# Normalising attention's outputs instead of its probabilities, and making the cell's gate rows later, in one kernel

## The chip, the cores and the metric

One Trainium2 chip, one core of it. The metric is the device time of one execution of the whole program, in microseconds; the median of the runs counts. All arithmetic is float32.

## The reference

Two blocks of two layers each work on 512 tokens of width 1024; the first block has 256 context tokens besides. A layer of the first block has three branches (a depthwise convolution of width 31, a gated linear attention, a grouped softmax attention) that are merged; a layer of the second block is an mLSTM cell and a retention in chunks. The parts that the change touches:

```python
def gqa_attend(q, k, v):
    s = jnp.einsum('bqkgd,bskd->bkgqs', q, k).astype(jnp.float32) * (ATT_HD ** -0.5)
    p = jax.nn.softmax(s, axis=-1).astype(v.dtype)
    return jnp.einsum('bkgqs,bskd->bqkgd', p, v)
...
    li = gate_chunks(i_pre.astype(jnp.float32))
    lf = gate_chunks(jax.nn.log_sigmoid(f_pre.astype(jnp.float32)))
...
        b = jnp.cumsum(lfj, axis=-1)
        a = b + m[..., None]
        g = b[..., :, None] - b[..., None, :] + lij[..., None, :]
...
        m_row = jnp.maximum(a, jnp.max(g, axis=-1))
        w_intra = jnp.exp(g - m_row[..., None])
```

Attention has 8 query heads and 2 key heads of width 64; the 512 latent tokens look at 768 keys, and in layer 0 the 256 context tokens look at their own 256. The gate rows are what the cell needs of i and f for its four heads along the 512 tokens: running sums, running maxima and their differences.

## The kernel before

Each engine has a program of its own (tensor, scalar, vector, gpsimd, sync), written out in order by hand. A wait names an event by a key (`at(("probs", i, e))`); a first pass of the program counts at which value of which semaphore the event happens. Every operation of VectorE and of GpSimd that goes through `link` waits for its own end. ScalarE's functions all go through line 1089, most of VectorE's through lines 1483 to 1489, so that the trace shows these helpers' lines and not the callers'.

PSUM has 8 banks of 128 x 512 floats. `claim` waits until the last reader of a bank has freed it. Weights come through a ring of four slots of 1 MB, loaded by the sync engine as slots are used up; attention uses none.

**Attention** (`attend`, lines 657, 1197 and 1638) walks over pairs: one pair is 128 queries of two heads e = 0, 1. Layer 0 has 8 pairs of context (256 keys, one half) and 16 of latents (768 keys, two halves of 384); layer 1 has the 16 of latents. Banks are taken by parity: pair i has banks 4(i mod 2) to 4(i mod 2)+3, one for each head and half. A round n does scores of pair n (L677, heads on different rows of TensorE), transposes of the probabilities of pair n-1 (L690) into the banks that held its scores, and values of pair n-2 (L711, heads on different columns) into columns 384 to 512 of a bank of the other parity. VectorE takes the negated maximum of a head's scores (L1651); ScalarE makes exponentials with it as bias, and their sum by the side (shown as a read of its accumulator); VectorE takes the reciprocal (L1489) and multiplies the probabilities by it (L1485), and only then does TensorE transpose. ScalarE copies three of the four transposed halves and the output from PSUM (L1089), VectorE the fourth (L1488). TensorE's order is: scores, transposes of head 0, values of the pair before, transposes of head 1. ScalarE's order is: copy (0,1), exponential of head 0, copy (0,0), output copy, copy (1,0), exponential of head 1.

Beside this, **GpSimd** convolves: 31 taps, each a multiply by a column (L1966) and an addition (L1967), for four tiles and in layer 0 for two segments. TensorE's first work after attention is the sum over the convolution's channels (`csum`, through L419), which waits for the whole convolution (`("conv", l)`, line 860). After attention VectorE multiplies all heads by their gate (line 1727), which waits for `("att out", l)`.

**The second block** has for each layer and head four or five groups of products (`steps2`, `products` and `corners`, lines 950 to 976): a 1024 x 256 weight load is multiplied in seven quarter-sized products of sums. `products` is four of them; VectorE then makes U2 from two results (line 1874) and W2 and the corner c22 (lines 1876 and 1892); `corners` (three products) waits for U2 and c22. After corners VectorE adds U2 to two quarters (lines 1897 to 1911). All of these products are at L947. GpSimd makes the sums of weights (`pair_sums`, L2003 to L2006), each set waiting for the corners of two groups before, and for the cell's heads a four-tap convolution (`taps`, L2019, L1966, L1967).

Ahead of all groups a narrow product with the gate weights is made (`("if", l)`, L435). **ScalarE** takes it from PSUM with two biases, then absolute value, exponential and logarithm (lines 1389 to 1395), and **VectorE**, which has just made the sums of h (lines 1802 to 1805), waits for the logarithm and makes the gate rows (lines 1806 to 1818): one two-input operation, two scans, four two-input operations and a small copy, all on 4 partitions of 512. TensorE wants the rows at `gate_cols` (line 920), after the fifth group of head 0. In VectorE's order the gate rows stand before the U2 of group (0, 0).

```python
                for n in range(len(pairs) + 1):
...
                    if n < len(pairs):
                        for e in range(2):
                            z = 2 * (i % 2) + e
                            eng.wait_ge(*at(("probs", i, e)))
                            rcp(small[:, 48 + z:49 + z], small[:, 44 + z:45 + z])
                            ts(pr[:, z, 0:halves * w], pr[:, z, 0:halves * w], small[:, 48 + z:49 + z], None, M_, None,
                               ("probs norm", i, e))
```

## Time and profile before

| | |
|---|---|
| runs | 3575.69, 3580.43, 3581.15 us; median 3580.43 |
| the profiled execution | 3579.02 us, its span 3577.0 us |
| busy: PE / DVE / ACT / POOL | 3259.3 / 1339.7 / 833.6 / 1433.7 us |
| chain that ended last | PE 73%, POOL 15%, DVE 7%, issue 3%, ACT 2% |
| attention of layer 0, first scores to the column sums | 583.86 to 739.72 us |
| attention of layer 1, first scores to the column sums | 1669.11 to 1770.65 us |
| second block, first groups of its layers | 2145.65 and 2872.76 us |

PE is TensorE's matmuls, PEld its weight loads, DVE VectorE, ACT ScalarE, POOL GpSimd. Times count from the span's start. A float32 matmul shows as two instructions, a transpose as one. The chain that ended last is followed back from the last instruction; its parts on POOL are the convolution's end of layer 0 and GpSimd's share at the beginning of the second block's layers. Where a timeline row has brackets at its end, the engine stood still for so long before it, and what follows the arrow is what ended the wait.

### The profile page before, as it was taken

What the parts mean: (1) busy time and instruction counts of PE and PEld (TensorE: products, weight loads), DVE (VectorE), ACT (ScalarE), POOL (GpSimd) and SP (SyncE); (2) the same over time, 40 slices, a digit from 0 to 9 for tenths busy, and PEclk for the clock granted to TensorE, in tenths of its full rate; (3) what the DMA queues carried; (4) which work ended last, traced back from release to release, by engine and by line L of the source; (5) the groups of instructions that cost most, each with busy time, mean ns of one, the idle gap of its engine ahead of it and who ended that gap; (6) DMA issues with size and microseconds to landing.
All of it is one profiled execution on the core that took longest, in us unless ns stands there. A gap on an engine that the chain in (4) does not pass through costs nothing.

```text
span 3577.0 us, 38442 instructions
## 1 busy us (share of the span) xinstructions
PE 3259.3 (91%) x14397; PEld 2221.3 (62%) x14397; DVE 1339.7 (37%) x2454; ACT 833.6 (23%) x1487; POOL 1433.7 (40%) x1372
## 2 busy tenths in 40 slices
PE   5999897779999989987899979999999889999998
PEld 4666564546665546454544437888986378889953
DVE  6211314724444231225632242555552234444322
ACT  2312323611111031323521112222121023221110
POOL 0008988920000000899200016667651166775600
PEclk6999997989999999998999989999999999999998
DMA  6111110003222111210034412322331321222211
GB/s 193 47 36 36 30 36 13 2 24 97 92 88 91 50 57 47 53 36 24 1 112 124 130 52 71 94 84 83 107 106 36 84 71 60 71 71 71 71 46 48
DMA packets 259178, 236.47 MB, mean 66 GB/s; under 512 B 20870, under 2 KB 257202, under 8 KB 258996
## 3 DMA queue, kind: packets, MB, share of 16 engines
q1 hardware_dynamic: 258996, 234.02, 21.5%
q8 instruction: 117, 1.92, 0.2%
q14 instruction: 65, 0.53, 0.0%
HBM read 231.90 MB, written 2.10 MB: 65 GB/s over the span
## 4 chain that ended last, share of the span: by engine, by line
PE 73%; POOL 15%; DVE 7%; issue 3%; ACT 2%; DMA 0%; DVEq 0%; ACTq 0%; SPq 0%; POOLq 0%
PE ps L419 33%; PE ps L947 20%; POOL arena L1967 8%; PE ps L449 8%; POOL posi L1966 4%; PE ps L997 2%; DVE arena L1483 2%; ACT arena L1089 1%; PE ps L435 1%; PE ps L1041 1%; DVE arena L1487 1%; PE ps L1033 1%; DVE bQz L1487 1%; PE ps L515 1%; DVE arena L1485 1%
## 5 line engine op out<-in xcount | busy, mean ns | idle before, releaser
L419 PE MATMUL ps<-hT,wring 128*128 128x512 f32 (+1 forms) x1568 | 579.2, 530 | 1.4 <-ACT arena L1089 1.4
L419 PE MATMUL ps<-arena,wring 128*128 128x512 f32 (+1 forms) x1280 | 489.9, 543 | 10.6 <-DVE arena L1483 10.6
L419 PEld LDWEIGHTS ps<-hT,wring 128*128 128x128 f32 x1568 | 303.5, 195 | 261.0 <-issue 244.9
L2003 POOL TENSOR_TENSOR arena<-wring 128x512 f32<-128x512 f32 x72 | 93.2, 1294 | 867.7 <-DMA wring<-in_w_in 561.8
L1967 POOL TENSOR_TENSOR arena<-arena,posi 128x512 f32<-128x512 f32 (+1 forms) x360 | 409.2, 1137 | 30.0
L449 PE MATMUL ps<-hT,wring 128*128 128x512 f32 (+1 forms) x1088 | 403.9, 525 | 0.0
L419 PEld LDWEIGHTS ps<-arena,wring 128*128 128x128 f32 x1280 | 242.7, 191 | 246.6 <-issue 227.2
L1089 ACT ACTIVATE arena<-ps 128x256 f32<-128x256 f32 (+4 forms) x447 | 194.1, 434 | 747.8 <-PE ps L419 324.9
L449 PEld LDWEIGHTS ps<-hT,wring 128*128 128x128 f32 x1088 | 205.8, 194 | 162.6 <-issue 153.3
L1089 ACT ACT_TABLE_LOAD x146 | 187.3, 1283 | 492.1 <-PE ps L527 95.2
L1483 DVE TENSOR_TENSOR arena<-arena 128x768 f32<-128x768 f32 (+7 forms) x121 | 158.2, 1307 | 363.4 <-ACT arena L1089 360.5
L1089 ACT ACTIVATE arena<-ps,cols 128x512 f32<-128x512 f32 (+2 forms) x186 | 113.4, 610 | 717.4 <-PE ps L419 404.0
L1966 POOL TENSOR_SCALAR posi<-arena,cols 128x512 f32<-128x512 f32 (+1 forms) x360 | 250.4, 695 | 35.4
L947 PE MATMUL ps<-hT,wring 128*128 128x256 f32 x896 | 228.3, 401 | 26.4 <-DVE posi L1483 26.2
L1979 POOL TENSOR_TENSOR arena<-arena 128x512 f32<-128x512 f32 (+1 forms) x12 | 13.1, 1092 | 521.4 <-ACT arena L1089 520.6
L1487 DVE SCALAR_TENSOR_TENSOR bQz<-wring,cT,bQz 128x256 f32<-128x256 f32 x392 | 213.9, 546 | 14.0
L947 PE MATMUL ps<-hT,arena 128*128 128x256 f32 x896 | 213.1, 381 | 0.0
L947 PE MATMUL ps<-xT,wring 128*128 128x256 f32 x896 | 211.7, 379 | 0.0
L947 PEld LDWEIGHTS ps<-hT,wring 128*128 128x128 f32 x896 | 175.8, 202 | 54.8 <-DVE posi L1483 29.2
L947 PEld LDWEIGHTS ps<-hT,arena 128*128 128x128 f32 x896 | 171.9, 192 | 24.0
L947 PEld LDWEIGHTS ps<-xT,wring 128*128 128x128 f32 x896 | 170.2, 190 | 23.1
L1973 POOL MEMSET arena<- 128x60 f32 x8 | 1.2, 151 | 447.1 <-DVE arena L1483 446.5
(184 smaller groups left out, 4300.9 us busy)
## 6 DMA issues: line engine op xcount, KB each, us to landing
wring<-in_w_in SPq DMA_DIRECT2D x128, 1024.0 KB, 5.3
wring<-in_w_mod SPq DMA_DIRECT2D x24, 1024.0 KB, 7.7
wring<-in_w_out SPq DMA_DIRECT2D x24, 1024.0 KB, 5.7
wring<-in_w_ada SPq DMA_DIRECT2D x24, 1024.0 KB, 5.2
wring<-in_w_conv_out SPq DMA_DIRECT2D x8, 512.0 KB, 3.6
wring<-in_w_gla_out SPq DMA_DIRECT2D x8, 512.0 KB, 4.0
wring<-in_w_attn_out SPq DMA_DIRECT2D x8, 512.0 KB, 4.0
arena<-in_x SPq DMA_DIRECT2D x1, 2048.0 KB, 9.6
```

The source lines that it names most:

```text
L419: last = eng.matmul(o_(out), a, b_, start=(i == 0), stop=(i == len(parts) - 1))
L435: mm = eng.matmul(bank[b][0:M, 0:n], w[:, k, 0:M], hT[:, k, t0:t0 + n], start=(k == 0), stop=(k == KD - 1))
L449: mm = eng.matmul(bank[b][:, 0:n], w[:, k, j * P:(j + 1) * P], hT[:, k, t0:t0 + n], start=(k == 0), stop=(k == KD - 1))
L515: last = eng.matmul(o_[:, c:c + 1], (md2 if L > 2 else md_first if (L, g) < (0, 8) else md)[:, i, c * 256 + j * P:c * 256 + (j + 1) * P], ...
L947: mm = eng.matmul(o_, lhs, rhs, start=first and u == 0 and k == 0, stop=k == 3, skip_group_check=True)
L997: eng.matmul(bank[7 - j][:, 0:TX], w_out[j][:, k, :], ys[:, k, :], start=(k == 0), stop=False)
L1089: act.link(eng.activation(out_, in_, func, **kw), key)
L1483: tt = lambda o_, a, b, op, key=None: dve.link(eng.tensor_tensor(o_, a, b, op), key)
L1487: eng.scalar_tensor_tensor(out=o_, in0=a, scalar=s_, in1=b, op0=op0, op1=op1), key)
L1966: pool.link(eng.tensor_scalar(scratch, src, w, 0.0, ALU.mult, ALU.add))
L1967: pool.link(eng.tensor_tensor(dst, dst, scratch, ALU.add))
L2003: pool.link(eng.tensor_tensor(t1, w[:, 0:4, P:2 * P], w[:, 0:4, 0:P], ALU.subtract))
```

## The change

Two parts in one kernel.

*Attention.* Probabilities are transposed and multiplied with the values as the exponentials are. VectorE makes one reciprocal of both heads' sums a pair. In the middle of the values of a pair, after the second tile of keys, TensorE spreads the reciprocals over a head's 64 rows by a product with the identity, into the neighbouring bank; VectorE copies this from PSUM (128 x 128), waits for the values and multiplies the output by it on its way out of PSUM, in place of ScalarE's copy. TensorE's order becomes scores, all four transposes, values; scores are made with half 1 first, and banks are claimed half by half. The values' bank is claimed, since it holds the transposes just made. ScalarE's order becomes three copies, two exponentials.

*Gate rows.* ScalarE's five functions stand after its copy for the corners of load (0, 0), VectorE's eight operations after the c22 of load (0, 1).

```diff
@@ tensor
+        osum = sq[1][:, 0:P]
...
-                    claim(b0, b0 + 1, b0 + 2, b0 + 3)
...
-                    for half in range(halves):
+                    for half in range(halves - 1, -1, -1):
+                        claim(b0 + half, b0 + 2 + half)
...
-                    eng.wait_ge(*at(("probs norm", i, e)))
+                    eng.wait_ge(*at(("probs", i, e)))
...
+                    claim(b)
                     g = hp // 2
                     for kt in range(halves * w // P):
                         for e in range(2):
                             last = eng.matmul(bank[b][rows_of[e], 384:512], av[:, kt, g * 64:(g + 1) * 64],
                                               pt[:, 2 * (i % 2) + e, kt * P:(kt + 1) * P],
                                               start=(kt == 0), stop=(kt == halves * w // P - 1))
+                        if kt == 1:
+                            claim(b + 1)
+                            eng.wait_ge(*at(("shares", i)))
+                            for e in range(2):
+                                z = 48 + 2 * (i % 2) + e
+                                spread = eng.matmul(bank[b + 1][rows_of[e], 384:512], small[:, z:z + 1].broadcast_to([P, 64]),
+                                                    ident, start=True, stop=True)
+                            spread.then_inc(*pe.tell(("full", part)))
...
                     if 1 <= n <= len(pairs):
-                        halves = key_halves(pairs[n - 1][0])[0]
-                        for half in range(halves - 1, -1, -1):
-                            turn(n - 1, 0, half, half > 0 or n == 1)
+                        for e in range(2):
+                            for half in range(key_halves(pairs[n - 1][0])[0]):
+                                turn(n - 1, e, half)
                     if n >= 2:
                         values(n - 2)
-                    if 1 <= n <= len(pairs):
-                        for half in range(halves):
-                            turn(n - 1, 1, half, True)
@@ scalar, attend
+                for n in range(len(pairs) + 1):
+                    if n:
+                        for half in range(key_halves(pairs[n - 1][0])[0]):
+                            turned(n - 1, 0, half)
+                        turned(n - 1, 1, 0)
                     if n < len(pairs):
                         probabilities(n, 0)
                         probabilities(n, 1)
@@ scalar, corners of the second block
                         if not r and i:
                             silu(n, i - 1)
+                        if (n, i) == (0, 0):
+                            gate_rows()
@@ vector, attend, after the maxima of pair n
+                    if 1 <= n <= len(pairs):
+                        if key_halves(pairs[n - 1][0])[0] > 1:
+                            k = ("pT", i - 1, 1, 1)
+                            eng.wait_ge(*at(("full", k)))
+                            cp(pt[:, 2 * ((i - 1) % 2) + 1, 384:768], bank_of[k][:, 0:384], ("free", k))
+                        z = 2 * ((i - 1) % 2)
+                        eng.wait_ge(*at(("probs", i - 1, 1)))
+                        rcp(small[:, 48 + z:50 + z], small[:, 44 + z:46 + z], ("shares", i - 1))
+                    if n >= 2:
...
+                        eng.wait_ge(*at(("full", part)))
+                        cp(osum, bank_of[part][:, 384:512], ("free", part))
                         eng.wait_ge(*at(("full", k)))
+                        tt(res[:, 8 + hp, q0:q0 + P], bank_of[k][:, 384:512], osum, M_, ("free", k))
@@ vector, products of the second block
                         tt(c22, d_, w_, A_, ("c22", k))
+                        if (n, i) == (0, 1):
+                            gate_rows()
```

## Rows read from the trace of the kernel before

**Rows 1.** Timeline, end of layer 0's attention: start us, us, engine, line, shapes, count, wait.

```profile
739.72 8.12 PE L419 MATMUL ps<-arena,const 128*128 128x512 f32 x16 [25.03 <-POOL arena L1967]
```

**Rows 2.** Groups by shape, GpSimd, 611 to 708 us: count, busy us, mean ns, idle.

```profile
L1967 POOL TENSOR_TENSOR arena<-arena,posi 128x512 f32<-128x512 f32 x30 | 40.3, 1343 | 2.5
L1966 POOL TENSOR_SCALAR posi<-arena,cols 128x512 f32<-128x512 f32 x30 | 22.9, 763 | 2.9
```

**Rows 3.** The same view, GpSimd, from 745 us to the end (second block).

```profile
L1967 POOL TENSOR_TENSOR arena<-arena 128x512 f32<-128x512 f32 x96 | 121.9, 1270 | 8.0
...
L1966 POOL TENSOR_SCALAR arena<-arena,cols 128x512 f32<-128x512 f32 x96 | 66.8, 696 | 9.3
```

**Rows 4.** Timeline, layer 1's attention: scores of rounds 3 and 15, column sums.

```profile
1689.73 1.56 PE L677 MATMUL ps<-arena 64*128 64x384 f32 x8 [1.03 <-DVE small L1489]
...
1758.86 1.56 PE L677 MATMUL ps<-arena 64*128 64x384 f32 x8 [1.03 <-DVE small L1489]
...
1770.65 3.70 PE L419 MATMUL ps<-arena,const 128*128 128x512 f32 x8
```

**Rows 5.** Timeline, one round of layer 1's attention.

```profile
1724.78 1.56 PE L677 MATMUL ps<-arena 64*128 64x384 f32 x8 [1.03 <-DVE small L1489]
...
1725.70 0.62 DVE L1485 TENSOR_SCALAR arena<-arena,small 128x768 f32<-128x768 f32 x1
...
1726.27 0.87 PE L690 MATMUL ps<-const,arena 128*128 128x128 f32 x6
1726.41 1.95 DVE L1651 TENSOR_REDUCE small<-ps 128x1 f32<-128x768 f32 x2
1726.91 0.49 ACT L1089 ACTIVATE arena<-ps 128x384 f32<-128x384 f32 x1 [1.51 <-PE ps L690]
...
1727.07 1.53 PE L711 MATMUL ps<-arena 128*64 128x128 f32 x24
1727.46 0.90 ACT L1089 ACTIVATE arena<-ps,small 128x768 f32<-128x768 f32 x1
...
1728.53 0.88 PE L690 MATMUL ps<-const,arena 128*128 128x128 f32 x6
1728.71 1.32 ACT L1089 ACTIVATE arena<-ps 128x384 f32<-128x384 f32 x3 [0.26 <-PE ps L711]
1729.51 0.56 DVE L1488 COPY arena<-ps 128x384 f32<-128x384 f32 x1 [1.16 <-PE ps L690]
```

**Rows 6.** Timeline, first groups of the second block's layers.

```profile
2145.82 1.40 ACT L1089 ACTIVATE arena<-ps,small 4x512 f32<-4x512 f32 x2 [4.26 <-PE ps L435]
...
2151.85 0.68 DVE L1487 SCALAR_TENSOR_TENSOR arena<-arena 4x512 f32<-4x512 f32 x1 [5.15 <-ACT arena L1089]
...
2158.58 3.52 PE L947 MATMUL ps<-hT,wring 128*128 128x256 f32 x8 [5.76 <-DVE posi L1483]
...
2165.73 1.29 POOL L2003 TENSOR_TENSOR arena<-wring 128x512 f32<-128x512 f32 x1 [48.91 <-PE ps L947]
...
2219.74 0.72 ACT L1089 ACTIVATE arena<-arena,cols 128x512 f32<-128x512 f32 x1 [3.29 <-POOL arena L1967]
...
2885.82 3.42 PE L947 MATMUL ps<-hT,wring 128*128 128x256 f32 x8 [5.89 <-DVE posi L1483]
```

**Rows 7.** Chain that ended last: start us, us, what.

```profile
2232.61 5.18 PE ps L947 x24
```

**Rows 8.** Windows of layer 1's attention: busy us by engine, PEclk, DMA share, GB/s.

```profile
1668.00:1690.00 22.00, 15.35 (x74) 9.98 (x76) 15.87 (x22) 10.11 (x19) 20.28 (x20) 0.64 0.00 1
...
1720.00:1765.00 45.00, 36.18 (x349) 26.03 (x346) 32.16 (x56) 29.75 (x64) 0.00 (x0) 1.00 0.00 1
```

**Rows 9.** Timeline, gate of layer 0's linear attention, GpSimd and VectorE.

```profile
399.99 2.13 DVE L1549 TENSOR_TENSOR_SCAN arena<-gscan,arena 128x768 f32<-128x768 f32 x1
400.60 2.57 POOL L1967 TENSOR_TENSOR arena<-arena,posi 128x512 f32<-128x512 f32 x1
```

More of the change, by code:

```diff
@@ L678, in scores, with turn @@
                                               ak[r, hp // 2, half * w:(half + 1) * w], start=True, stop=True)
-                            if half == halves - 1:
+                            if half == 0:
                                 last.then_inc(*pe.tell(("scores", i, e)))
-                def turn(n, e, half, tell):
+                def turn(n, e, half):
                     i = first + n
@@ L691, in turn @@
                                              pr[:, 2 * (i % 2) + e, half * w + u * P:half * w + (u + 1) * P], ident)
-                    if tell:
-                        last.then_inc(*pe.tell(("full", key)))
+                    last.then_inc(*pe.tell(("full", key)))
                 def values(n):
@@ L698, in values @@
                     halves, w = key_halves(sg)
-                    key = ("o", i)
+                    key, part = ("o", i), ("shares", i)
                     b = 4 * ((i + 1) % 2)
-                    if n == len(pairs) - 1:
-                        claim(b)
-                    bank_of[key], last_on[b] = bank[b], key
                     for e in range(2):
@@ L713, in values @@
                                               start=(kt == 0), stop=(kt == halves * w // P - 1))
-                    last.then_inc(*pe.tell(("full", key)))
-                    if n < len(pairs) - 1:
-                        m.mark(("full", ("pT", i + 1, 0, 0)), *m.at[("full", key)])
+                        if kt == 1:
[6 more added lines that the diff above has]
+                            spread.then_inc(*pe.tell(("full", part)))
+                    if halves > 1:
+                        last.then_inc(*pe.tell(("full", key)))
+                    else:
+                        m.mark(("full", key), *m.at[("full", part)])
+                    bank_of[key], bank_of[part] = bank[b], bank[b + 1]
+                    last_on[b], last_on[b + 1] = key, part
                 for n in range(len(pairs) + 2):
@@ L1218, in turned @@
                     evac(("pT", i, e, half), pt[:, 2 * (i % 2) + e, half * w:(half + 1) * w], 0, w)
-                def output(n):
-                    sg, hp, qb = pairs[n]
-                    q0 = SEG[sg][0] + qb * P
-                    evac(("o", first + n), res[:, 8 + hp, q0:q0 + P], 384, P)
-                for n in range(len(pairs) + 2):
-                    before = key_halves(pairs[n - 1][0])[0] if 1 <= n <= len(pairs) else 0
-                    if before == 2:
-                        turned(n - 1, 0, 1)
+                for n in range(len(pairs) + 1):
[3 more added lines that the diff above has]
+                        turned(n - 1, 1, 0)
                     if n < len(pairs):
                         probabilities(n, 0)
-                    if before:
-                        turned(n - 1, 0, 0)
-                    if n >= 2:
-                        output(n - 2)
-                    if before:
-                        turned(n - 1, 1, 0)
-                    if n < len(pairs):
                         probabilities(n, 1)
-                m.mark(("att out", l), *m.at[("free", ("o", first + len(pairs) - 1))])
             for l in range(DEPTH):
@@ L1642, in attend @@
                 att_no[0] += len(pairs)
-                for n in range(len(pairs) + 1):
+                for n in range(len(pairs) + 2):
                     i = first + n
@@ L1651, in attend @@
                             dve.link(eng.tensor_reduce(small[:, 40 + z:41 + z], src, ax, ALU.max, negate=True), ("nmax", i, e))
-                    if n and key_halves(pairs[n - 1][0])[0] > 1:
-                        k = ("pT", i - 1, 1, 1)
-                        eng.wait_ge(*at(("full", k)))
-                        cp(pt[:, 2 * ((i - 1) % 2) + 1, 384:768], bank_of[k][:, 0:384], ("free", k))
-                    if n < len(pairs):
-                        for e in range(2):
-                            z = 2 * (i % 2) + e
-                            eng.wait_ge(*at(("probs", i, e)))
-                            rcp(small[:, 48 + z:49 + z], small[:, 44 + z:45 + z])
-                            ts(pr[:, z, 0:halves * w], pr[:, z, 0:halves * w], small[:, 48 + z:49 + z], None, M_, None,
-                               ("probs norm", i, e))
+                    if 1 <= n <= len(pairs):
[7 more added lines that the diff above has]
+                    if n >= 2:
+                        sg, hp, qb = pairs[n - 2]
+                        q0 = SEG[sg][0] + qb * P
+                        k, part = ("o", i - 2), ("shares", i - 2)
+                        eng.wait_ge(*at(("full", part)))
+                        cp(osum, bank_of[part][:, 384:512], ("free", part))
+                        eng.wait_ge(*at(("full", k)))
+                        tt(res[:, 8 + hp, q0:q0 + P], bank_of[k][:, 384:512], osum, M_, ("free", k))
+                m.mark(("att out", l), *m.at[("free", ("o", first + len(pairs) - 1))])
             for l in range(DEPTH):
```

44 lines of the change are left out of this document (24 added, 20 removed).

## Prediction

> **What bounds the kernel now.** I read three places: the windows for what each engine does in a stretch, the timeline of one round of each loop that the diff touches, and the timeline where the next stage picks up. What decides there is which wait ends last, not which engine is busy.
>
> Attention of layer 0 is not on the path. When it ends, TensorE stands still for 25.03 us until GpSimd has finished the depthwise convolution; the column sums start at 739.72 [rows 1]. The path there is GpSimd's, and the normalising multiplies of VectorE slow it: while they run, its 512-wide multiply takes 763 ns and its 512-wide add 1343 ns [rows 2], against 696 and 1270 ns later, with no such neighbour [rows 3].
>
> Attention of layer 1 is on the path: its column sums follow the last values at 1770.65 without a gap [rows 4]. One round of it shows what sets its pace [rows 5]. TensorE has scores from 1724.78, the transposes of the even head from 1726.27, values from 1727.07, the transposes of the odd head from 1728.53, together 4.61 us, and then waits for about 1.0 us; the round lasts 5.65. The ring that closes it is ScalarE's exponential of the odd head (0.90 and 0.19 for its sum), VectorE's reciprocal and multiply (0.16, 0.62), the maximum of the next pair (half of 1.95), the exponential of its even head (1.1), and the three copies that stand before the odd one in ScalarE's order (1.32): 5.3 us before any signalling. The multiply stands in this ring. While GpSimd still convolves, multiply and GpSimd lengthen each other, so the mean of the 12 rounds from 1689.73 to 1758.86 is 5.76 us [rows 4].
>
> In both layers of the second block VectorE makes the gate rows, from 2151.85, ahead of the sum U2 that TensorE's first corner product needs; TensorE waits 5.76 us and restarts at 2158.58, slowly: eight matmuls in 3.52 us, 24 until 2165.57 [rows 6]. At full clock such 24 take 5.18 [rows 7]. When they end GpSimd starts on the third load (2165.73) and is at work until it releases ScalarE at 2219.74 [rows 6]. The second layer is the same, with 5.89 us waited [rows 6].
>
> **The change, part by part.**
> 1. *Layer 1's attention.* Out of VectorE go two multiplies and one of two reciprocals a pair; in come a copy and a product of 128x128 from PSUM. Neither form is in the trace; the 128x384 copy takes 0.56 [rows 5], so each lies between a third of that, 0.19, and the whole. I take 0.3. VectorE then has 1.95 + 0.56 + 0.16 + 0.6 = 3.3 us of work a round; ScalarE loses its output copy (0.28 or so of the 1.32) and has 1.04 + 0.5 + 2.2 = 3.7. TensorE gains four half instructions of the value kind: 24 of these take 1.46 us [rows 5], so 0.24 (bounds 0.2 and, with their own signalling, 0.5). Its work is 4.61 + 0.24 = 4.85.
>  New waits: values now wait, after all four transposes, for ScalarE's copies of the first two. The copy of the first starts 0.64 after the transposes do, as now [rows 5], and takes 0.49, so 1.1, plus up to 0.35 of signalling; the four transposes take 1.6. The second copy is done at 1.65 and is wanted at 1.6 + 0.5 = 2.1. Both are hidden, if ScalarE has finished its exponentials by then; it has more than 1 us to spare. Queued behind this wait are the next scores. These now wait for VectorE's copy of the spread sums: maxima end 2.1 after the transposes' start, then odd-head copy 2.7, reciprocal 2.9, spread copy 3.2, with signalling 3.4 to 3.6, against the values' end at 3.3. That is 0.1 to 0.3 of stall. The product that frees the output bank ends at 3.9 and is covered by the first half of the scores (0.75). Exponentials end at 4.2 and the next transposes begin at 5.1: hidden. So the ring is now TensorE's own: 4.85 + 0.2 stall + 0.15 for the break in the middle of values = 5.2 us, bounds 4.9 and 5.5. Twelve rounds: 12 x (5.76 - 5.2) = 6.7 us.
>  Head: the transposes of pair 0 start without reciprocal and multiply, 1.2 us earlier for the second head (two of 0.16 + 0.62, less what the exponential between them takes), and the first slow rounds carry 1.5 in all. The granted clock is 0.64 there [rows 8], so TensorE's added work costs double and I do not take more. Tail: no multiply before the last transposes, an added product after the last values that the column sums don't need: 1.3. Together 9.5 us (bounds 5 and 13).
> 2. *Layer 0's attention.* Its own shortening, some 12 us, buys nothing: TensorE would wait 37 instead of 25 us. What is gained is GpSimd's time: 30 x (1343 - 1270) ns + 30 x (763 - 696) ns = 4.2 us [rows 2, 3]; with the 256-wide operations in the last third of the stretch, for which I add a quarter, 5.3 (bounds 3 and 6). The new VectorE operations read PSUM; I charge GpSimd nothing for them.
> 3. *Gate rows.* At their old place they cost the wait and the slow restart. Moved, U2 is ready when the first four product groups end (2158.58 - 5.76 = 2152.82), the corner ends 5.18 later at 2158.0 instead of 2165.57: 7.5 us earlier, and GpSimd's chain with it. ScalarE's five gate functions with two table loads take 6.0 us, from 2145.82 to where VectorE starts on their result [rows 6]; from 2154.9, after the corner's first copy, they end at 2160.9, and the next group needs ScalarE at 2161.5. VectorE's now stand ahead of the corner sums of load 1, which free a bank wanted only ten us later.
>  But they now run beside GpSimd, which is the path there. Beside a scan of 2.13 us GpSimd's addition of 1.27 took 2.57, so it lost 0.61 of VectorE's time [rows 9, 3]. Gate rows are 6.2 us of such operations (2151.85 to 2158.1), but on 4 partitions; rows show no price for so few. Bounds: nothing, and all of the 6.2. By the scan's share it would be 3.8; I take 3.4, since half of them are shorter operations with a gap behind each. Net 7.5 - 3.4 = 4.1 to 4.2, in two layers 8.3 (bounds 2.6 and 15).
>  The Trainium skill (GPSIMD Engine Reference, Specifications) says the SBUF interfaces are shared with VectorE, with contention from VectorE instructions in a 2-port mode or with two SBUF inputs. By that rule the removed multiplies help and the moved gate rows hurt, which [rows 2, 3, 9] bear out; it gives no size.
>
> **Sum.** 9.5 + 5.3 + 8.3 = 23.1. The profiled execution took 3579.0 (span 3577.0), 1.4 below the median of 3580.4; from the median that is 3557.
>
> **Rivals.**
> - *GpSimd pays for the gate rows in full.* The moved rows cost it 5.5 to 7.5 us a layer, since VectorE is also slowed and the moved group grows to 9 us. Then part 3 gives 0 to 4 and the time is 3561 to 3566. For: GpSimd is on the path throughout [rows 6, 9]. Against: only four partitions. Chance 0.15.
> - *The round is not shortened*: values wait for ScalarE's copies and the next scores for VectorE's, and it stays near 5.6. Part 1 gives 3 to 4; 3563. For: two new waits a round. Against: the slack above. Chance 0.12.
> - *Gate rows cost GpSimd nothing and rounds run at 4.9*: 13 + 6 + 15 = 34, 3546. Chance 0.08.
> - *Slower: the clock stays low.* TensorE's granted clock in layer 1's first 22 us is 0.64, after which it is 1.00 [rows 8]; the levels are 1.2 and 2.4 GHz. Should the new waits keep it at the lower level, a round of 4.85 us of work takes 9.7, 4.5 more than forecast. From five such rounds more than now the 23 us are gone, with all 13 it is 3615. Against: TensorE is busy for 93% of the new round, 82% of the old. Chance 0.03.
> - *It does not do what it says*: the moved functions leave U2 late by another wait, as the first copy on ScalarE is queued behind norm work, and only parts 1 and 2 remain: 3566. Against: ScalarE had been idle for 4.26 us when it took up the gate functions [rows 6]. Chance 0.04.
>
> The forecast has 0.52, and 0.06 stays for what I don't see: 0.04 that it ends within 0.2% (7 us, about what a measurement of this kernel tells from no change), 0.02 that it is slower. With 0.01 of the last rival's 0.04, same has 0.05; slower has 0.03 + 0.02; faster the rest, 0.90. Range 3544 to 3570: from just below the best bounds of all three parts to the rounds not shortened or GpSimd paying in full, and most of both together.
>
> **What would show it.** Layer 1: score matmuls 5.2 us apart, and 9 to 10 us from the first scores to the column sums gone. Layer 0: the wait for GpSimd grows to some 31 us, while the column sums start 5 us earlier. GpSimd's wide operations back at 696 and 1270 ns there. Second block: no wait before the corner; GpSimd's operations stretched for some 8 us beside the gate rows, ScalarE released about 4 us earlier against the block's start. Wrong if rounds take 5.6, if the scans leave GpSimd alone, or if GpSimd's convolution ends when it does now.

## The result and the profile after

The changed kernel takes 3548.16 us (median of four, 3545.75 to 3549.36) against 3580.79 on the same chip: ratio 0.9914, 95% interval 0.9902 to 0.9926. That is 32.6 us faster; 3557 was forecast. The profiled execution took 3549.07 us, its span 3547.0 us, 30.0 less than before's. In the new listing the scores are L678, transposes L691, values L709, the spread product L717, the column sums L420, the second block's products L953, ScalarE's functions L1095; VectorE's two-input operations are L1482 and its copies L1487; GpSimd's taps are L1976 and L1977.

The timeline of TensorE shows how the two attentions end, and the first scores and those of rounds 3 and 15 of layer 1, to be held against [rows 1, 4]:

```profile
732.58 8.21 PE L420 MATMUL ps<-arena,const 128*128 128x512 f32 x16 [29.99 <-POOL arena L1977]
...
1658.58 0.92 PE L678 MATMUL ps<-arena 64*128 64x384 f32 x4
1661.61 2.21 PE L678 MATMUL ps<-arena 64*128 64x384 f32 x12 [2.12 <-DVE arena L1482]
...
1678.62 1.56 PE L678 MATMUL ps<-arena 64*128 64x384 f32 x8
...
1738.20 1.56 PE L678 MATMUL ps<-arena 64*128 64x384 f32 x8 [0.25 <-DVE arena L1487]
...
1747.99 3.70 PE L420 MATMUL ps<-arena,const 128*128 128x512 f32 x8
```

Layer 0's column sums come 7.1 us earlier, though TensorE waits 5 us longer for them. In layer 1 they come 22.7 us earlier, 15.5 of it beyond layer 0's. Of these 9.6 are the twelve rounds from 3 to 15 (69.13 us became 59.58) and 2.0 the tail behind round 15 (11.79 became 9.79). The other 4.0 lie ahead of round 3. Before, the first scores stood in one group:

```profile
1669.11 5.06 PE L677 MATMUL ps<-arena 64*128 64x384 f32 x16 [3.03 <-DVE arena L1483]
```

Now four of the sixteen matmuls run at 1658.58, inside the wait for VectorE, since banks are claimed by halves. The other twelve start at 1661.61, 7.5 us earlier than before's. From the first scores to the column sums it takes 89.4 us instead of 101.5: 12.1 gone, where 9 to 10 were forecast.

GpSimd by shape, 611 to 708 us, against [rows 2]:

```profile
L1977 POOL TENSOR_TENSOR arena<-arena,posi 128x512 f32<-128x512 f32 x30 | 38.2, 1272 | 2.5
L1976 POOL TENSOR_SCALAR posi<-arena,cols 128x512 f32<-128x512 f32 x30 | 20.8, 693 | 2.9
```

Both are at the undisturbed durations of [rows 3]. One round of layer 1, against [rows 5]:

```profile
1703.43 1.56 PE L678 MATMUL ps<-arena 64*128 64x384 f32 x8 [0.25 <-DVE arena L1487]
...
1704.92 1.53 PE L691 MATMUL ps<-const,arena 128*128 128x128 f32 x12
1705.06 1.95 DVE L1650 TENSOR_REDUCE small<-ps 128x1 f32<-128x768 f32 x2 [1.48 <-PE ps L678]
1705.56 1.54 ACT L1095 ACTIVATE arena<-ps 128x384 f32<-128x384 f32 x3 [1.36 <-PE ps L691]
...
1706.38 0.66 PE L709 MATMUL ps<-arena 128*64 128x128 f32 x8
...
1706.87 0.39 PE L717 MATMUL ps<-const,small 128*64 128x128 f32 x4
...
1707.08 1.04 PE L709 MATMUL ps<-arena 128*64 128x128 f32 x16
1707.13 0.90 ACT L1095 ACTIVATE arena<-ps,small 128x768 f32<-128x768 f32 x1
1707.64 0.17 DVE L1488 RECIPROCAL small<-small 128x2 f32<-128x2 f32 x1
1707.84 0.29 DVE L1487 COPY arena<-ps 128x128 f32<-128x128 f32 x1
...
1708.24 0.29 DVE L1482 TENSOR_TENSOR arena<-ps,arena 128x128 f32<-128x128 f32 x1
...
1708.42 0.92 PE L678 MATMUL ps<-arena 64*128 64x384 f32 x4 [0.30 <-DVE arena L1487]
```

TensorE has no gap but the one ahead of the scores, and that one waits for VectorE's copy of the spread sums. Scores are 4.95 to 5.0 us apart, 4.97 in the mean of the twelve rounds.

The beginning of the second block, against [rows 6], ScalarE left out:

```profile
2137.11 1.30 POOL L2013 TENSOR_TENSOR arena<-wring 128x512 f32<-128x512 f32 x1 [41.63 <-PE ps L953]
...
2144.22 0.69 POOL L1976 TENSOR_SCALAR arena<-arena,cols 128x512 f32<-128x512 f32 x1
...
2144.87 0.68 DVE L1486 SCALAR_TENSOR_TENSOR arena<-arena 4x512 f32<-4x512 f32 x1
2145.00 1.69 POOL L1977 TENSOR_TENSOR arena<-arena 128x512 f32<-128x512 f32 x1
2145.59 2.18 DVE L1818 TENSOR_TENSOR_SCAN arena<-arena 4x512 f32<-4x512 f32 x1
2146.78 1.48 POOL L1976 TENSOR_SCALAR arena<-arena,cols 128x512 f32<-128x512 f32 x1
2147.80 1.53 DVE L1819 TENSOR_TENSOR_SCAN arena<-gscan,arena 4x512 f32<-4x512 f32 x1
2148.35 2.05 POOL L1977 TENSOR_TENSOR arena<-arena 128x512 f32<-128x512 f32 x1
2149.36 2.68 DVE L1482 TENSOR_TENSOR arena<-arena 4x512 f32<-4x512 f32 x2
2150.49 1.01 POOL L1976 TENSOR_SCALAR arena<-arena,cols 128x512 f32<-128x512 f32 x1
...
2194.68 0.72 ACT L1095 ACTIVATE arena<-arena,cols 128x512 f32<-128x512 f32 x1 [1.62 <-POOL arena L1977]
```

The first products start at 2124.59, so GpSimd starts on the third load 12.5 us behind them, 20.1 before: the wait is gone and 7.6 us with it. ScalarE is released 70.1 us behind them, 74.1 before. GpSimd has thus lost 3.6 of the 7.6, and the rows show where: its multiply of 0.70 us takes 1.48, its addition of 1.27 takes 2.05 beside gate rows, and these take VectorE 10.8 us instead of 6.2.

The marks account for the profile's 30.0 us: 7.1 in layer 0, 15.5 in layer 1's attention, 1.6 lost again up to the second block's products, 4.0 in the first of its layers and 4.6 in the second; 0.4 lie elsewhere.

### The profile page after: what moved, and what is told of

Its sections match the earlier page's. It is cut to its first block, busy times and chain, and to the rows that moved or that the text cites. A ratio compares the mean times of both kernels' runs of the same rounds, so it can differ in the third digit from the quotient of the medians.

```text
span 3547.0 us, 38760 instructions
## 1 busy us (share of the span) xinstructions
PE 3262.0 (92%) x14557; PEld 2232.0 (63%) x14557; DVE 1299.8 (37%) x2414; ACT 822.2 (23%) x1447; POOL 1431.1 (40%) x1372
## 4 chain that ended last, share of the span: by engine, by line
PE 73%; POOL 15%; DVE 7%; issue 2%; ACT 2%; DMA 0%; DVEq 0%; ACTq 0%; SPq 0%; POOLq 0%
PE ps L420 34%; PE ps L953 21%; POOL arena L1977 8%; PE ps L450 8%; POOL posi L1976 4%; PE ps L1003 2%; DVE arena L1482 2%; PE ps L436 1%; PE ps L1047 1%; ACT arena L1095 1%; DVE arena L1486 1%; PE ps L1039 1%; DVE bQz L1486 1%; PE ps L516 1%; DVE small L1650 1%
## 5 line engine op out<-in xcount | busy, mean ns | idle before, releaser
L420 PE MATMUL ps<-hT,wring 128*128 128x512 f32 (+1 forms) x1568 | 577.0, 528 | 1.4 <-ACT arena L1095 1.4
L420 PE MATMUL ps<-arena,wring 128*128 128x512 f32 (+1 forms) x1280 | 491.1, 544 | 10.6 <-DVE arena L1482 10.6
L420 PEld LDWEIGHTS ps<-hT,wring 128*128 128x128 f32 x1568 | 303.2, 195 | 258.6 <-issue 242.4
L1977 POOL TENSOR_TENSOR arena<-arena,posi 128x512 f32<-128x512 f32 (+1 forms) x360 | 405.5, 1126 | 30.1
L420 PEld LDWEIGHTS ps<-arena,wring 128*128 128x128 f32 x1280 | 243.2, 191 | 247.3 <-issue 227.9
L1095 ACT ACTIVATE arena<-ps 128x256 f32<-128x256 f32 (+4 forms) x407 | 183.0, 450 | 748.0 <-PE ps L420 335.9
L1482 DVE TENSOR_TENSOR arena<-arena 128x768 f32<-128x768 f32 (+7 forms) x121 | 160.8, 1329 | 364.5 <-ACT arena L1095 361.2
L1095 ACT ACTIVATE arena<-ps,cols 128x512 f32<-128x512 f32 (+2 forms) x186 | 113.4, 610 | 720.5 <-PE ps L420 405.4
L1976 POOL TENSOR_SCALAR posi<-arena,cols 128x512 f32<-128x512 f32 (+1 forms) x360 | 244.9, 680 | 35.4
L953 PE MATMUL ps<-hT,wring 128*128 128x256 f32 x896 | 227.9, 400 | 19.4 <-DVE posi L1482 19.4
L953 PE MATMUL ps<-hT,arena 128*128 128x256 f32 x896 | 212.3, 380 | 0.0
L953 PE MATMUL ps<-xT,wring 128*128 128x256 f32 x896 | 211.7, 379 | 0.0
L953 PEld LDWEIGHTS ps<-hT,wring 128*128 128x128 f32 x896 | 175.1, 201 | 47.5 <-DVE posi L1482 22.2
L953 PEld LDWEIGHTS ps<-hT,arena 128*128 128x128 f32 x896 | 171.2, 191 | 23.9 <-issue 0.3
L953 PEld LDWEIGHTS ps<-xT,wring 128*128 128x128 f32 x896 | 170.2, 190 | 23.2
```

Of the source, the lines that this page charges most:

```text
L420: last = eng.matmul(o_(out), a, b_, start=(i == 0), stop=(i == len(parts) - 1))
L953: mm = eng.matmul(o_, lhs, rhs, start=first and u == 0 and k == 0, stop=k == 3, skip_group_check=True)
L1095: act.link(eng.activation(out_, in_, func, **kw), key)
L1482: tt = lambda o_, a, b, op, key=None: dve.link(eng.tensor_tensor(o_, a, b, op), key)
L1976: pool.link(eng.tensor_scalar(scratch, src, w, 0.0, ALU.mult, ALU.add))
L1977: pool.link(eng.tensor_tensor(dst, dst, scratch, ALU.add))
```

## The experiments

Each stands beside runs of the kernel before on its chip. The marks that tell parts apart are the column sums of the two layers, a round of layer 1 (mean of the twelve from round 3 to 15), and in the second block the time from the products' start to ScalarE's release (share 1) and, in its second layer, from the narrow gate product's start to the matmuls that wait for ScalarE's last release (share 2).

| kernel | median us, ratio [95%] | column sums 0, 1 | round | share 1, 2 |
|---|---|---|---|---|
| before | 3580.79 | 739.72, 1770.65 | 5.76 | 74.1, 84.3 |
| changed | 3548.16, 0.9914 [0.9902, 0.9926] | 732.58, 1747.99 | 4.97 | 70.1, 79.7 |
| changed again | 3547.27, 0.9901 [0.9885, 0.9918] | 733.49, 1748.84 | 4.96 | 70.1, 79.7 |
| attention alone | 3560.49, 0.9947 [0.9932, 0.9962] | 733.47, 1748.85 | 4.96 | 74.4, 84.5 |
| gate rows alone | 3567.72, 0.9969 [0.9957, 0.9981] | 739.84, 1769.23 | 5.72 | 70.7, 80.6 |
| multiplies back | 3599.26, 1.006 [1.0043, 1.0077] | 743.61 | 7.36 | 70.1 |
| multiplies last | 3563.73, 0.9951 [0.9936, 0.9966] | 739.54, 1764.27 | 5.42 | 70.1 |
| order alone | 3563.95, 0.9968 [0.9952, 0.9985] | 740.96, 1759.81 | 5.06 | 74.1, 84.4 |
| claim in one piece | 3552.38, 0.9926 [0.9911, 0.9941] | 734.08, 1753.87 | 5.32 | 70.1 |
| copy first | 3543.24, 0.9896 [0.9881, 0.9910] | 734.77, 1745.54 | 4.75 | 70.0 |
| gate rows early | 3537.37, 0.9883 [0.9867, 0.9898] | 732.78, 1746.00 | 4.96 | 67.7, 77.3 |
| the same again | 3543.41, 0.9894 [0.9877, 0.9910] | 732.79, 1748.53 | 4.97 | 67.7, 77.3 |
| more rows | 3566.73, 0.9966 [0.9953, 0.9979] | 735.07, 1752.56 | 4.96 | 77.8, 88.2 |
| both steps | 3542.87, 0.9896 [0.9882, 0.9911] | 733.25, 1748.18 | 4.76 | 67.6, 77.3 |

**The two parts by themselves.** First, the gate rows stand where they stood:

```diff
-                def gate_rows():
-                    act.stage("cell_gates")
+                act.stage("cell_gates")
...
-                        if (n, i) == (0, 1):
-                            gate_rows()
```

> The attention part alone; the gate rows stay at their old place. The change made 32.6 us (3580.8 to 3548.2). In its trace 7.1 us of that were there when layer 0's column sums began and 22.7 when layer 1's did, 21.1 at the first products of the second block. If the two parts add up, this kernel gains those 21 us, 3559 to 3560, and its column sums of layer 1 start at 1748.0 as with both parts. Rival: the 1.6 us lost between layer 1's attention and the second block belong to the gate rows' part; then the products start 22.7 us earlier, at 2123.0, and the time is 3558. Rival: what was gained later in the second block comes from attention as well; then it is below 3555.

Then the kernel before, with the calls of `gate_rows` where the change puts them:

> The gate rows' part alone; attention as before. From the trace of the changed kernel the corner comes 7.6 us earlier in a layer against its products, GpSimd loses 3.6 of these beside the gate rows, and later marks show 5 to 10 us in both layers together. My theory: 7 to 10 us gained, 3571 to 3574, GpSimd's share of the first layer (from the corner's end to ScalarE's release) 57.6 us instead of 54.0. Rival: parts interact, and alone it gives under 4 us, above 3576.

Attention alone gains 18.5 us, gate rows alone 11.2, more than the 7 to 10 expected; GpSimd's share is 57.6 us as expected. The product of the two ratios is 0.9916, the change has 0.9914: within the intervals the parts add. The 1.6 us lost between layer 1's attention and the second block appear with attention alone (column sums to products 376.7 us; 375.1 with gate rows alone), but the repeats below show the same difference between two runs of one kernel, so it isn't shown to be attention's doing.

**The multiplies put back.** Ahead of the transposes VectorE multiplies each head's probabilities by ones, first ahead of the spread copy in its order, then behind the output product:

```diff
-                    eng.wait_ge(*at(("probs", i, e)))
+                    eng.wait_ge(*at(("probs again", i, e)))
...
+                    if n < len(pairs):
+                        for e in range(2):
+                            z = 2 * (i % 2) + e
+                            eng.wait_ge(*at(("probs", i, e)))
+                            ts(pr[:, z, 0:halves * w], pr[:, z, 0:halves * w], ones[:, 0:1], None, M_, None, ("probs again", i, e))
```

> The changed kernel, with VectorE multiplying each head's probabilities by a column of ones ahead of their transposes; the outputs are still scaled at the end. If the removed multiplies are what GpSimd gains in layer 0, its wide operations return from 1272 and 693 ns to about 1343 and 763, and layer 0's column sums from 732.6 to 738 or later. If the multiply in the ring set the round of layer 1, rounds return from 4.97 us to 5.5 or more (0.62 us for each head in the ring, the first of which is hidden), which is 7 us or more in 12 rounds. Together with a longer head, 15 to 22 us slower than the changed kernel: 3563 to 3570. Rival: the round is shorter only because transposes stand together and banks are claimed by halves; then rounds stay at 5.0, GpSimd's gain alone is lost, and it is 3554 to 3555.

> VectorE multiplies each head's probabilities by a column of ones ahead of their transposes, as in the run with the multiplies put back, but now behind the output product in VectorE's order; there they stood ahead of the copy of the spread sums, which the next scores wait for, and rounds took 7.03 us. Theory A: that run's 2.07 us a round came from the place, and the multiply itself costs a round only what VectorE's work then exceeds TensorE's by: 4.5 us of VectorE work with gaps against 4.97, so rounds of 5.0 to 5.3. Theory B, the prediction's: the multiply stood in a ring with the exponentials, and its removal is what shortened the round; then rounds return to 5.5 or more, as before the change. In both, GpSimd is as slow as before in layer 0 (about 1335 and 767 ns) and its column sums come at 737 to 740. By A 3553 to 3558, by B 3560 to 3564.

GpSimd's wide operations return to 1330 and 767 ns in the first, 1346 and 767 in the second. With the multiplies last the column sums of layer 0 are back at 739.54 as well: layer 0's gain is theirs. (In the first, attention of layer 0 itself ends only at 743.6, later than GpSimd, at 738.3.)

Layer 1 answered otherwise than either text had it. In the first place a round takes 7.36 us in the mean and 7.03 once GpSimd has finished, far more than its two multiplies: they wait for the exponentials, and the spread copy, for which the next scores wait, is queued behind them. The 3599 us are outside both expectations; the profiled execution, of which the marks are, was the fastest of the four (3586.1, the others 3598.5 to 3602.5). At the end of VectorE's order the round depends on GpSimd: the time, 3563.7, is theory B's, the mean round of 5.42 us neither's. Scores of that kernel, TensorE's timeline:

```profile
1712.57 1.56 PE L678 MATMUL ps<-arena 64*128 64x384 f32 x8 [0.75 <-DVE arena L1487]
...
1718.02 1.56 PE L678 MATMUL ps<-arena 64*128 64x384 f32 x8 [0.74 <-DVE arena L1487]
...
1724.03 1.56 PE L678 MATMUL ps<-arena 64*128 64x384 f32 x8 [0.75 <-DVE arena L1487]
...
1728.99 1.56 PE L678 MATMUL ps<-arena 64*128 64x384 f32 x8 [0.25 <-DVE arena L1487]
...
1733.94 1.56 PE L678 MATMUL ps<-arena 64*128 64x384 f32 x8 [0.26 <-DVE arena L1487]
```

and the two multiplies of a round, VectorE's timeline, beside GpSimd and after it:

```profile
1718.12 2.56 DVE L1484 TENSOR_SCALAR arena<-arena,const 128x768 f32<-128x768 f32 x2
...
1744.04 1.30 DVE L1484 TENSOR_SCALAR arena<-arena,const 128x768 f32<-128x768 f32 x2
```

While GpSimd convolves, the twelve rounds take 5.4 to 6.3 us. As soon as it has finished, at 1720.3, they come down to 4.95, as in the changed kernel, with both multiplies still in them.

**The order alone.** Hence the other half of it: the kernel before with the change's order of work, and probabilities still normalised. ScalarE, not shown, makes its three copies ahead of the first exponential and its output copy between the two.

```diff
-                    claim(b0, b0 + 1, b0 + 2, b0 + 3)
-                    for half in range(halves):
+                    for half in range(halves - 1, -1, -1):
+                        claim(b0 + half, b0 + 2 + half)
...
+                        for e in range(2):
+                            for half in range(key_halves(pairs[n - 1][0])[0]):
+                                turn(n - 1, e, half)
                     if n >= 2:
                         values(n - 2)
-                    if 1 <= n <= len(pairs):
-                        for half in range(halves):
-                            turn(n - 1, 1, half, True)
```

> The kernel before, with the change's order of work in attention and nothing else of it: TensorE does scores (half 1 first, banks claimed by halves), all four transposes, values; ScalarE three copies, exponential of head 0, the output copy, exponential of head 1. VectorE still normalises the probabilities, each head by itself; gate rows at their old place. Theory A, from the run with the multiplies put last (4.95 us a round once GpSimd had finished): the order shortened the round and not the multiply's removal; rounds after 1730 go from 5.65 to 5.0 to 5.2 us, and beside GpSimd they take 5.5 to 6. Layer 0 gains nothing, 739 to 740. Layer 1's attention ends 6 to 10 us earlier: 3570 to 3575. Theory B, the prediction's: rounds stay at 5.6 since reciprocal and multiply stand between the exponential and the transposes: 3578 to 3581.

Theory A holds for the rounds and B is refuted; A's time, 3570 to 3575, was too cautious. Layer 0 gains nothing (740.96). The timeline of a round, exponentials and maxima left out in part:

```profile
1744.50 1.56 PE L677 MATMUL ps<-arena 64*128 64x384 f32 x8 [0.33 <-DVE arena L1478]
1744.59 0.90 ACT L1082 ACTIVATE arena<-ps,small 128x768 f32<-128x768 f32 x1
1744.59 0.62 DVE L1475 TENSOR_SCALAR arena<-arena,small 128x768 f32<-128x768 f32 x1
...
1745.88 0.62 DVE L1475 TENSOR_SCALAR arena<-arena,small 128x768 f32<-128x768 f32 x1
...
1746.00 1.53 PE L690 MATMUL ps<-const,arena 128*128 128x128 f32 x12
```

The scores hide the first head's multiply; the second head's ends at 1746.50, in time for the six of the twelve transposes that need it. From 1725.16 to 1749.22 five rounds take 24.06 us, 4.81 each, with every multiply and reciprocal in place; 5.65 before [rows 5] and 4.97 in the changed kernel, which has the spread product besides. The twelve rounds together take 60.8 us: the order alone brings 8.4 of the change's 9.6. The kernel takes 3563.95 us, a median 16.9 below before's (the ratio's interval holds 5 to 17). What moving the normalisation adds to this is read between this kernel and attention alone: the column sums come 7.5 us earlier in layer 0 and 11.0 in layer 1, so 3.5 in layer 1, 1.2 of it in the twelve rounds. By their times alone the two can't be told apart (0.9968 and 0.9947, intervals overlap).

Where the old order lost its time stands in [rows 5]. TensorE stands still once a round, 1.03 us before the scores, which claim all four banks of their parity. The last of these is freed by VectorE's copy, 1729.51 to 1730.07, which itself waited 1.16 us for the second head's transposes, and these came last in TensorE's order. ScalarE's three copies end only 0.04 us before it. (The row names the reciprocal behind the copy as the one that ended the wait; the scores don't take its result.) The multiply of the second head's probabilities, 1725.70 to 1726.32, had ended 2.2 us before the transposes that take them, at 1728.53. In the new order values stand behind the transposes and hide this copy; 0.2 to 0.3 us of the wait are left.

**The banks' claim in one piece:**

```diff
-                        claim(b0 + half, b0 + 2 + half)
+                        if half == halves - 1:
+                            claim(b0, b0 + 1, b0 + 2, b0 + 3)
```

> The changed kernel, but the scores of a pair wait for all four banks at once before the first of them. My theory: claims by halves hide VectorE's product that frees the output bank behind the first half of the scores (0.75 us). With the claim in one piece the scores start 0.3 to 0.6 us later in each round, which goes from 4.97 us to 5.3 to 5.5, and the first rounds lose some more: 4 to 8 us slower than the changed kernel, 3552 to 3556, of which 2 to 4 us at the beginning of layer 1's attention, where the clock is low. Rival: the claims by halves buy nothing, since VectorE's order keeps both halves waiting for the same product: within 1 us of 3548.

A round takes 5.32 us, 0.35 more; the wait ahead of the scores is 0.62 us and is for the output product, no longer for the copy. Twelve rounds are 4.2 us, and the median is 4.2 above the changed kernel's, though the ratios' intervals overlap. The other half of the text failed: the first rounds lost nothing; from the last product before attention to round 3 it took 18.7 us instead of 21.1. The granted clock of the 20 us from 1660 was 0.83 there and 0.74 in the changed kernel.

**The spread copy ahead of the reciprocal** (VectorE's two operations change places):

> The changed kernel with one step moved: VectorE copies the spread sums of the pair before ahead of the reciprocal and not after it. The scores wait 0.25 us a round for this copy. Theory: the wait is the 0.17 us reciprocal and its gap, so the round goes from 4.97 to 4.75 us and the attention of layer 1 ends 2 to 3 us earlier: 3545 to 3546. Rival: the round is TensorE's own work and another wait (its transposes for ScalarE's exponentials) takes the place: rounds 4.9 to 4.97, 3547 to 3549.

The scores' wait is gone and a round takes 4.75 us, TensorE's own work. In twelve rounds that is 2.5 us. The median, 3543.2, is just under the text's 3545 to 3546 and 4.0 below the changed kernel's on that chip, but their intervals overlap.

**The gate rows one group earlier** (ScalarE's five functions at their old place):

```diff
-                        if (n, i) == (0, 1):
+                        if (n, i) == (0, 0):
                             gate_rows()
```

> The changed kernel, with the gate rows made one group earlier: ScalarE's gate functions at their old place, VectorE's eight operations after U2 and c22 of group (0, 0), that is mostly before GpSimd begins on the third load. Theory: GpSimd's 3.6 us of loss in each layer come from its running beside the gate rows; here it runs beside a third of them at most and loses 1.3 us or less, 2 us less a layer, 3543 to 3545. Rival: VectorE makes the sums of group (0, 1) late, the corner waits for them, and what GpSimd wins TensorE loses: 3547 to 3551.

Share 1 is 67.7 us, share 2 77.3: 2.4 less in each layer. GpSimd, from its start at 2133.15 to ScalarE's release at 2188.10, takes 54.95 us against 57.57 in the changed kernel and 54.01 before: of its loss 0.9 is left. The corner doesn't wait. The theory holds and not the rival; but the median was 9.9 us lower than the changed kernel's beside it, twice what this explains, and the intervals overlap.

**More gate rows** (one of VectorE's 4-partition operations nine times):

> The changed kernel, with one of the gate rows' two-input operations (4 partitions of 512, 0.68 us by itself) made nine times instead of once, beside GpSimd. It prices such an operation on 4 partitions for GpSimd. Theory: the price does not go by partitions; for each microsecond of VectorE's two-input operations GpSimd loses about a third to a half, so eight more of 0.68 us cost it 2 to 3.5 us beyond the 3.6, in each layer, 4 to 7 us in all: 3551 to 3555. Rival: operations on so few partitions cost GpSimd nothing and the 3.6 us come from the two scans alone: GpSimd's share stays at 57.6 us and the time within 1.5 us of 3548 (TensorE has slack until the sums of load 1 are wanted).

Gate stretch, both engines' timelines:

```profile
2153.99 13.96 DVE L1482 TENSOR_TENSOR arena<-arena 4x512 f32<-4x512 f32 x10
...
2157.90 1.60 POOL L2014 TENSOR_TENSOR arena<-wring 128x512 f32<-128x512 f32 x1
2159.58 1.60 POOL L2015 TENSOR_TENSOR arena<-wring,arena 128x512 f32<-128x512 f32 x1
2161.26 1.59 POOL L2016 TENSOR_TENSOR wring<-wring 128x512 f32<-128x512 f32 x1
...
2172.15 3.79 PE L953 MATMUL ps<-wring,hT 128*128 128x128 f32 x16 [11.35 <-DVE posi L1482]
```

This is the contention at rest. An operation on 4 partitions takes VectorE 1.40 us instead of 0.68, and GpSimd's addition takes 1.60 instead of 1.27: it loses 0.33 of every 1.7 us. The rival (few partitions cost nothing) is out. Over the same 22 operations GpSimd takes 32.5 us, 30.5 in the changed kernel: 2.0 more, the lower end of the 2 to 3.5 expected. The time was missed, 3566.7 for 3551 to 3555. TensorE was not free to be kept waiting: the next corner's sums are queued behind the gate rows and it waited 11.35 us, 0.69 in the changed kernel. GpSimd then stood still for 5.8 us until that corner was done. These 5.8 and the 2.0 are the 7.7 by which share 1 grew: at that length most of the price is TensorE's wait.

**Both steps**, and the changed kernel and the early gate rows again:

> The changed kernel with the two steps that gained, together: the copy of the spread sums ahead of the reciprocal (rounds of 4.75 us) and the gate rows one group earlier (GpSimd loses 0.9 us a layer and not 3.6). By mechanism they are worth 2.5 us and 4.9 us, 3547.3 less 7.4: 3538 to 3542. If they add as measured (4.0 and 9.9 us), 3533 to 3534; if the 3537.4 of the earlier gate rows had luck in how the clock returned after waits, 3540.

> The changed kernel again, on the chip of the three runs beside it, so that they can be held against it: 0.991 of before, 3546 to 3551. Layer 0's column sums within 1 us of 732.6, rounds of layer 1 4.96 to 4.97 us.

> The kernel with the gate rows one group earlier once more. It took 3537.4 us, 9.9 less than the changed kernel beside it, where its mechanism accounts for 4.9; and with the copy moved as well, which shortens every round by 0.2 us, it took 3542.9. Theory A: where the granted clock comes back after a wait is fixed by a kernel's own timing; the same kernel then takes 3536 to 3540 again, and its first scores of layer 1 start at 1661 with the clock at 0.91 in the 20 us before 1660. Theory B: it differs from run to run or chip to chip by a few us; then this run falls nearer to the 3542 that the mechanism gives (3540 to 3545), and marks of the profile move against each other by 2 us or more.

Theory B holds for the repeat. The same kernel took 3536.6 to 3537.9 in three runs and 3544.7 in the fourth on one chip, and 3542.7 to 3544.3 on another. Shares and rounds agree within 0.1 us; what differs is the granted clock around the waits. The windows of its two profiles, 1660 to 1680 and 2030 to 2050 us, where the third value from the end is the granted clock; first the one of 3537:

```profile
1660.00:1680.00 20.00, 16.19 (x104) 9.88 (x106) 14.83 (x21) 11.26 (x22) 18.45 (x18) 0.83 0.00 1
...
2030.00:2050.00 20.00, 15.40 (x33) 6.57 (x32) 5.12 (x5) 1.02 (x2) 0.00 (x0) 0.91 0.19 63
```

and the one of 3543:

```profile
1660.00:1680.00 20.00, 13.21 (x78) 9.47 (x80) 12.44 (x16) 10.18 (x19) 18.36 (x19) 0.74 0.00 1
...
2030.00:2050.00 20.00, 15.40 (x30) 6.45 (x29) 4.53 (x4) 1.19 (x2) 0.00 (x0) 0.83 0.32 105
```

From the first scores to round 3 one takes 15.4 us and the other 20.0; but the first scores of the one start 2.2 us later, so that 2.4 are left between layer 0's column sums and round 3. From layer 1's column sums to the second block's products it is 374.4 and 376.6. Together that is 4.6 of the 6.8 us between the two spans.

By mechanism both steps should bring 7.4 us; 4.4 were measured, 3542.9 against 3547.3, a higher time than in any of the text's three cases. Against the changed kernel's 0.9901 and 0.9914 the 0.9896 is not shown to be faster. What is shown of the two steps is their own rows.

## Why the forecast was right in sign and 9 us too high

- **Layer 0, forecast 5.3 us: right.** The mechanism is shown by the multiplies put last. The column sums come 4.7 to 7.1 us earlier in the nine traces that leave the multiplies out, 6.1 in the mean; TensorE waits 30.0 us where 31 was said.
- **Gate rows, forecast 7.5 less 3.4 a layer: right.** Measured 7.6 less 3.6. Few partitions did not lower the price, and shorter operations cost less than scans, as was assumed: GpSimd's three operations from 2145.00 to 2150.40, beside which the two scans run, lost 2.0 us (0.42, 0.78 and 0.78), and the long row of two-input operations cost it 0.33 of every 1.68 us. In the second layer share 2 has 4.6 instead of 4.1. Alone it measured 11.2 (8.3 forecast); the shares account for 3.4 + 3.7 = 7.1 of it, and the rest is open, of the size that the clock moves.
- **Layer 1's attention, forecast 9.5: the term that was too small; 15.5 measured.** The twelve rounds gave 9.6 for 6.7, the tail 2.0 for 1.3, the head 4.0 where 1.5 was taken. The round was priced at 5.2. It has 4.95: TensorE's own work is 4.75 (copy first), not 4.85, the stall for the spread copy 0.20 as forecast, and the 0.15 added for the break in the values was not there.
- **The step that failed is a reason, not a number: "The multiply stands in this ring."** [rows 5] show that TensorE waited for neither multiply; the second head's had ended 2.2 us before it was wanted. TensorE's round closed over its own 4.61 us of work and VectorE's copy of the last transposes. In the ring that was named ScalarE's copies stood 0.26 us waiting for the values [rows 5], so it was not the one that closed. With the change's order and the multiplies kept, a round takes 4.81, less than the changed kernel's 4.97. Moving the normalisation saves GpSimd's time in layer 0 and frees the early rounds of layer 1 from the mutual slowing; once GpSimd has finished it gives layer 1's rounds nothing. That the forecast round came near the measured one is thus partly luck: the new order's waits were worked out rightly, what they replaced was not. How much of the order's gain is the place of the transposes, how much ScalarE's order and how much the claim by halves no run separates; in the changed kernel the claim is worth 0.35 us a round.
- **The rivals.** That the round stays near 5.6 is out; that gate rows cost GpSimd all, or nothing, too. The best case had rounds of 4.9 and, with 3546, came closer to the median than the forecast; but its condition that gate rows cost GpSimd nothing did not hold. "The clock stays low" is out for the rounds (granted 1.00 from 1683 us on), and the head, 1661 to 1683 us, had 0.77 where 0.64 stood [rows 8]. Where the granted clock differs between profiles, the head and the stretches behind later waits differ by a few microseconds.
- **What stays open.** Of the head's 4.0 us, how much is the change's. From layer 0's column sums to round 3 it takes 950.0 and 949.0 us in the two traces with the old attention, and 943.9 to 948.1 in the nine with the new one and without the multiplies; the early gate rows' two profiles differ by 2.4 with the same instructions. So one profile can't tell.

## What to carry to other kernels

Before taking an operation out of a ring, look in the timeline when its result was ready and when it was first used: here it lay ready for 2.2 us, and what the path waited for was a copy that another order hides. What an engine off the path reads and writes in SBUF is paid by GpSimd if GpSimd is on it; price it by duration beside duration, not by partitions. And where a step is worth under 0.2%, read its own rows, since the clock's return after waits moves the whole by as much.

## What the runs showed of the hardware that was not expected

- VectorE and GpSimd slow each other on 4 partitions as on 128: 4x512 with 1.40 us instead of 0.68 beside 128x512 with 1.60 instead of 1.27. Two multiplies of 128x768 took 2.56 us beside GpSimd and 1.30 without. Even a copy of 4x3 took 1.12 us beside GpSimd (timeline of the changed kernel, 2152.08), 0.16 without. The Trainium skill (GPSIMD Engine Reference, Specifications) names VectorE instructions with two SBUF inputs as a source of contention, and the traces agree; but it gives no size. Another page of the Trainium skill (SBUF — State Buffer, SBUF: two separate sides) has the port as an exclusive lock, held for the whole instruction, under which the other stands still. Here the two overlap: in the 1.68 us of one addition with its gap, 1.27 alone, VectorE makes 1.2 operations of 0.68 alone, together 2.09 us of work, so they can't have taken turns by whole instructions. The measurement decides.
- VectorE's new operations, which read PSUM, left GpSimd at 1272 and 693 ns in layer 0, its undisturbed values.
- One kernel, unchanged, has two times 6 us apart: medians of 3537.4 and 3543.4 on two chips, and on the first of them one execution of four at 3544.7. The windows of the two profiles show the granted clock at 0.83 and 0.74 in the same 20 us, the instructions being the same. The Trainium skill (TensorE: Matmul & The Clock Gate, Part 1) says that how much is done at the lower clock varies from run to run; the traces agree, and here the two medians differ by 0.17%.
